# First tile's heads first in the key stage, two query blocks moved to the gather stage, inputs loaded at once

## The reference, cut to what matters

```python
q = (xc @ wq).reshape(C, 8, 2, 128)              # 16 half-heads of 128
s = einsum('chpd,hpnd->chpn', q, sub_keys)       # 128 scores a half-head
s1, i1 = top_k(s[:, :, 0], 16); s2, i2 = top_k(s[:, :, 1], 16)
top, pos = top_k((s1[..., :, None] + s2[..., None, :]).reshape(C, 8, 256), 16)
g = softmax(top)                                 # 8 heads x 16 = 128 experts a token
a = gelu(einsum('chkd,cd->chk', u_tab[eidx], xc))
out = einsum('chk,chkd->cd', g * a, v_tab[eidx])
```

## Time and profile before

| | us |
|---|---|
| runs timed (3) | 3694.53 median, 3687.42 to 3694.57 |
| profiled execution | 3679.2 |
| its span, first to last instruction | 3677.4 |
| TensorE's mean granted clock | 0.870 of full |

### The profile page before, as it was taken

The page is one execution under the profiler, slowest core; times in us unless marked ns, Lnnn a source line. Parts: engine busy times, 40 slices in busy tenths (PEclk is TensorE's granted clock), DMA queues, the critical chain, the costliest instruction groups (busy, mean ns, idle before and its releaser), DMA issues. The chain is left out here.

```text
span 3677.4 us, 30576 instructions
## 1 busy us (share of the span) xinstructions
PE 2689.4 (73%) x8773; PEld 1376.5 (37%) x8773; DVE 2342.6 (64%) x5334; ACT 694.0 (19%) x1885; POOL 1482.5 (40%) x1582
## 2 busy tenths in 40 slices
PE   6998676766697666863086886197417799999998
PEld 3445532223372232211022472042102265566555
DVE  1233877778876778789855468887886536433542
ACT  1021100312122200310022220022002213410341
POOL 0000365665546655676664006656666600000000
PEclk8999878986899878886599987599658999999999
DMA  8656699999999999999998349999999953234322
GB/s 307 240 194 225 248 403 389 352 360 333 400 360 369 355 395 403 363 370 360 370 368 311 105 151 378 407 387 381 383 407 364 362 207 132 92 138 141 141 92 75
DMA packets 345650, 1086.52 MB, mean 295 GB/s; under 512 B 32657, under 2 KB 41357, under 8 KB 338189
## 3 DMA queue, kind: packets, MB, share of 16 engines
q0 software_dynamic: 227216, 849.45, 60.4%
q1 hardware_dynamic: 118268, 235.12, 18.1%
HBM read 1080.21 MB, written 4.24 MB: 295 GB/s over the span
## 5 line engine op out<-in xcount | busy, mean ns | idle before, releaser
L2447 ACT ACTIVATE heads<-common,dots 128x128 f32<-128x128 f32 x768 | 277.9, 396 | 731.3 <-PE psum L2463 359.0
L1214 PE MATMUL psum<-ring,turned 128*128 128x512 f32 (+1 forms) x800 | 356.1, 598 | 75.0 <-issue 56.5
L2503 POOL DMA_INDIRECT lent<-in_peer_u_dram,picks_u x274 | 258.2, 942 | 351.2 <-DVE picks_u L2199 168.1
L2413 DVE SCALAR_TENSOR_TENSOR lent<-lent,psum 128x1024 f32<-128x1024 f32 x274 | 325.1, 1218 | 41.2 <-issue 20.5
L2463 PE MATMUL psum<-proj,heads 128*128 128x512 f32 x374 | 207.0, 655 | 181.4 <-DVE turned L2413 129.1
L2463 PE MATMUL psum<-lent,heads 128*128 128x512 f32 x524 | 285.6, 653 | 70.8 <-DMA lent<-in_peer_v_dram,picks_u 24.1
L2503 POOL DMA_INDIRECT lent<-in_peer_v_dram,picks_u x262 | 248.0, 947 | 133.8 <-issue 63.7
L1884 PE MATMUL psum<-ring,turned 128*128 128x512 f32 x512 | 243.1, 635 | 39.4 <-issue 13.4
L2421 DVE SCALAR_TENSOR_TENSOR psum<-lent,dots,psum 128x512 f32<-128x512 f32 x262 | 197.9, 755 | 101.4 <-DMA lent<-in_peer_v_dram,picks_u 55.0
L1214 PEld LDWEIGHTS psum<-ring,turned 128*128 128x128 f32 x800 | 161.5, 204 | 265.5 <-issue 253.3
L2413 DVE SCALAR_TENSOR_TENSOR proj<-proj,psum 128x1024 f32<-128x1024 f32 x195 | 232.7, 1218 | 37.7 <-issue 13.8
(11 more groups left out here) (416 smaller groups left out, 4698.3 us busy)
## 6 DMA issues: line engine op xcount, KB each, us to landing
ring<-in_w_in_dram SPq DMA_DIRECT2D x37, 2048.0 KB
ring<-in_peer_wq_dram SPq DMA_DIRECT2D x10, 2048.0 KB
lent<-in_w_in_dram SPq DMA_DIRECT2D x9, 2048.0 KB, 8.4
ring<-in_w_out_dram SPq DMA_DIRECT2D x9, 2048.0 KB
proj<-in_ada_w_dram POOLq DMA_DIRECT2D x14, 1024.0 KB, 6.7
heads<-in_ada_w_dram POOLq DMA_DIRECT2D x13, 1024.0 KB, 7.1
gate_rows<-in_ada_w_dram POOLq DMA_DIRECT2D x13, 1024.0 KB, 7.1
lent<-in_w_out_dram SPq DMA_DIRECT2D x5, 2048.0 KB, 8.1
```

The source lines that it names most:

```text
L1214: mm = pe.matmul(psum[:, b % nb, 0:cols], lhs(k, it), w[:, kk, :], start=k == 0, stop=k == k_total - 1)
L2413: dve.scalar_tensor_tensor(out=src, in0=src, scalar=1.0, in1=kept_row, op0=ALU.mult, op1=ALU.mult, accum_out=weight).then_inc(rows_used.se ...
L2447: act.activation(diags[n % DIAGS], ident, ACT.Copy, scale=dots[:, j:j + 1]).then_inc(diag_ready.sem, 1)
L2503: pool.indirect_dma_start(out=row_slot(r), out_offset=None, in_=tables_dram[which], in_offset=bass.IndirectOffsetOnAxis(ap=picks_u[:, t, j ...
```

## The change

1. **Setup.** SP issues the two x tiles right after `common`, then the small rows, then the two ctx tiles, then the ring loads; before, x and ctx were issued at the start of the ada stage and SP waited for them before the fourth ada load. The fourth ada load gets a place of its own (`proj`), so that all four are issued in the setup stage. The squares of all tiles, the scaling and the turning of stream 0 move into the setup stage. All 23 small loads are issued in the projection stage. Of 16 modulating steps DVE now makes ten and ACT six (8 and 8 before).
2. **Modulation pairs.** Projection (1,3,5,7) to (3,6,9,12); attention (4,18) to (4,9,14,18); output projection (1,3) to (1,2,3); norm (0) and key stage (3,8) to none.
3. **Key stage** for stream 0 (`TILE_FIRST`): 24 items in six groups; the groups that turn the rows back are put behind items 15, 17, 19 and 21; the last picks are made at the stage's end.
4. **`queries_left`**: heads 8 to 15 of tile 1 as a guest at the start of the experts stage; query blocks 2 and 3 are released there.
5. **Row slots.** Three (five) rows are issued as soon as the first picks are known, four more once block 0 is used; slots 4, 5 and 10 are held until `queries_left` is done.

```diff
+    beside_ring[len(plan) - 1] = (RING, proj[:, 0:SLOT], None, False)
...
             sp.dma_start(common, io["common"]).then_inc(*packs_loaded.one(16))
+            for t in range(2):
+                sp.dma_start(stream[:, t, :], io["x"][0, t * P:t * P + P, :]).then_inc(*latents_loaded.one(16))
...
+    TILE_FIRST = ((0, 0), (1, 0), (1, 1), (2, 0), (0, 1), (3, 0))
+    LEFT_OVER = (2, 3)
+    BLOCK_FIRST = ((0, 0), (1, 0), (2, 0), (3, 0), (3, 1))
...
-        split = (3,)
-        items = [(4 * b + j, t, n) for b in range(4) for t, n in (((0, 1), (1, 1)) if b in split else ((0, 2),)) for j in range(4)]
+        order = BLOCK_FIRST if hosted() else TILE_FIRST
+        items = [(4 * b + j, t, 1 if (b, 1) in order else 2) for b, t in order for j in range(4)]
...
+        rows_at = [15 + 2 * n for n in range(len(rows_back))]
...
+                if i in rows_at:
+                    turn_row_back(pe, rows_at.index(i))
             dot(pe, last)
-            turn_rows_back(pe)
+            used.extend(freed[b] for b in range(4) if hosted() or b not in LEFT_OVER)
...
+            if not hosted():
+                pair_indices(dve, 2 * s, PEER_HEADS - 2)
+                dve.wait_ge(*step_v.now())
+                write_picks(dve, l, 2 * s, 2 * TOPK, PICKS)
...
+    def queries_left(l):
...
+        heads_left = [4 * b + j for b in LEFT_OVER for j in range(4)]
...
+                for k in range(KD):
+                    mm = pe.matmul(psum[:, i % 3, 0:P], w[:, k, (h % 4) * P:(h % 4) * P + P], turned_s[0][:, k, P:2 * P],
+                                   start=k == 0, stop=k == KD - 1)
...
+                yield 2.0, asked_at(i)
...
+    HELD = (4, 5, 10)
+    first_order, all_order = [6, 7, 8, 0, 1, 2, 3, 9], [2, 3, 4, 5, 6, 7, 8, 0, 1, 9]
+    late_order = [6, 7, 8, 11, 12, 0, 1, 2, 3, 9]
...
-        quads.host(project_, (1, 3, 5, 7))
+        quads.host(project_, (3, 6, 9, 12))
...
-        quads.host(attend, (4, 18))
+        quads.host(attend, (4, 9, 14, 18))
...
-        quads.host(out_, (1, 3))
-        quads.host(norm, (0,))
+        quads.host(out_, (1, 2, 3))
+        quads.host(norm)
         wq0 = len(used) + 1
-        quads.host(keys, (3, 8), then_rows=lambda pool: rows_beside_keys(pool, wq0, 4))
+        quads.host(keys, then_rows=lambda pool: rows_beside_keys(pool, wq0, 3, 7))
```

More of the change, by code:

```diff
@@ L553, in sync @@
                     r += n
+            for t in range(2):
+                sp.dma_start(stream[:, 2 + t, :], io["ctx"][0, t * P:t * P + P, :]).then_inc(*loaded.one(16))
             issue_loads(sp)
@@ L775, in scalar @@
             act.wait_ge(*read_a.at(4))
-            for k in range(KD):
+            for k in range(2, KD):
                 x = turned_s[1][:, k, :]
@@ L2051, in vector @@
             dve.wait_ge(*step_v.now())
+            if not hosted():
+                pair_indices(dve, 2 * s, PEER_HEADS - 2)
+                dve.wait_ge(*step_v.now())
+                write_picks(dve, l, 2 * s, 2 * TOPK, PICKS)
         def first_of(h):
-            return items.index((h, 0, 1 if h // 4 in split else 2))
+            return min(i for i, (head, t0, _) in enumerate(items) if head == h and t0 == 0)
         def asked_at(i):
@@ L2080, in scalar @@
                        .then_inc(*read_a.one())
-            for n, (t, g) in enumerate(rows_back):
-                act.wait_ge(*products.at(4 + dots_at(last) + n + 1))
-                act.copy(mixed_v[:, t, 512 * g:512 * g + 512], psum[:, n, :]).then_inc(*scaled.one())
+                if i - 1 in rows_at:
+                    n = rows_at.index(i - 1)
+                    t, g = rows_back[n]
+                    act.wait_ge(*turned_back.at(n + 1))
+                    act.copy(mixed_v[:, t, 512 * g:512 * g + 512], psum[:, 6 + n % 2, :]).then_inc(*copied_back.one())
             if l == 1:
@@ L2089, in keys_stage @@
         if l == 0:
-            lifted_free[s] = products.now()
+            lifted_free[0] = products.now()
     heads_hi = heads[:, 2048:4096]
@@ L2526, in experts_stage, with gather @@
         gather_count[0] += 1
-        def gather(pool, row, tile0, first, picked0, early):
+        def gather(pool, row, tile0, first, picked0, early, held=None):
             r, back = first + row, row_before[first + row]
+            if held and slot_no[r] in HELD and slot_no[r] not in slot_no[first:r]:
+                pool.wait_ge(*held)
             t, which, j = tile0 + row // (2 * PICKS), row // PICKS % 2, row % PICKS
@@ L2547, in gpsimd @@
             for row in range(ahead, 4 * PICKS):
-                gather(pool, row, 2 * s, first, picked0, s == 0)
+                gather(pool, row, 2 * s, first, picked0, s == 0, left_done[-1] if len(left_done) > left_before else None)
             if follows is not None:
```

241 lines of the change are left out of this document (139 added, 102 removed).

## The result

The changed kernel takes 3754.34 us (median of 4 runs, 3740.38 to 3760.61) against 3694.16 of before (4 runs): ratio 1.0162, 95% interval 1.0131 to 1.0193. It is slower by 60 us; the forecast was 23 us slower and its range ended at 3733.

What follows compares the result with a forecast made beforehand. The prediction took DMA to bound the gather stages, PE the stretch from 50 to 409 us, loads the first 50. Its terms summed to +23.1 us on the profiled 3679.2, giving 3702.3, or 3717.6 for a median; range 3692 to 3733.

Steps and rivals of the forecast that it cites:

- Part 1, the start: Up to the projection's first pair: earlier loads, fewer ACT columns and no wait for that pair's load, -12.4 us in sum.
- Part 2, the pairs: Modulation pairs at new places: +7.7 us in projection and branch stages, +6.6 in attention, +2.0 in output projection.
- Part 3, the key stage: Layer 0's key stage: blocks 2 and 3 stay 256 wide, opening copy +1.3 us, DMA late by +2.9.
- Part 4, the two loads: Two weight loads a layer go in beside the gathered rows: +2.5 us in layer 0, +9.3 in layer 1.
- Part 5: Layer 1's key stage and experts opening: same items, no pair to drop, row 10 waits for row 0's use, +4.5 us.
- Narrow blocks: Rival, key stage: blocks 2 and 3 are only 128 columns wide, saving 15.1 us a layer, -7.1 in sum; chance 0.08.
- DMA has room: Rival, first 50 us of rows: DVE or POOL sets the pace, the loads cost nothing, +8.5 us in sum; chance 0.14.
- Pairs covered: Rival, projection, branches and attention: PE waits anyway, so the pairs' waits cost 14.3 us less, +8.8 in sum; chance 0.10.
- Held slots late: Rival, experts stage: `queries_left` stays at the lower clock, held slots come 9 us late a layer, +41 in sum; chance 0.08.

Runs made afterwards that it cites:

- start_only: The kernel before with the new start (the diff's "Setup" parts) alone; pairs, key stage and row slots as before: 3565.64 us against 3569.77, ratio 0.9992.
- the second pair of traces: Both kernels unchanged, measured once more on one chip: kernel before 3691.09 us in its one run, changed kernel 3754.18 against 3696.24, ratio 1.0172.
- the first comparison: The changed kernel against the kernel before, as first measured and traced: 3754.34 us against 3694.16, ratio 1.0162.
- narrow: The changed kernel with key-stage blocks 2 and 3 made 128 columns wide for tile 0 alone: 3594.69 us, ratio 1.0068 to the kernel before.
- late_loads: Changed kernel without `queries_left`, full ring, no seam, query blocks 2 and 3 released in the gather stage by a tiny guest: 3724.81 us, 1.0057 of before.
- the first group: Experiments made on one chip with the kernel before (3569.8 us there): new start alone, start with pairs, changed kernel without `queries_left`, and with narrow items.
- seam_in_before: The kernel before with the seam alone: row 643 takes slot 9, which row 639 has just taken: 3709.70 us against 3697.26, ratio 1.0039.
- after_again: The changed kernel, unchanged, measured once more on the same chip as the kernel before: 3754.18 us against 3696.24, ratio 1.0172.
- start_pairs: The kernel before with the new start and the modulation pairs at their new places; key stage and row slots as before: 3578.89 us, ratio 1.0019.
- before_again: The kernel before, unchanged, measured once more for a trace from the experiments' chip: 3691.09 us in its one run.

## Why the prediction was right in sign and wrong in size

**Part 1, the start: right.** Forecast -11.1 by the start of the projection (10.1 + 1.0), measured -12.0. The first pair, three groups into the projection, does not wait (products at 61.56 and 62.44 us), as forecast (-1.3). With the old places the loads that the start brings forward meet the first pair's: start_only shows that half of the gain is lost at once. The forecast had not asked what the earlier start makes late.

**Part 2, the pairs: the failed step, mis-sized.** "Back-to-back pairs stall PE 4.5 us" took the shortest landing, 5.0 us. The load took 8.1, and the stall was 7.60; the one in the branch stage was 1.60, less than the 2.6 forecast. The granted clock was 0.57 over the stretch behind, with products of nearly twice the time, which the sum had nowhere. Up to the key stage the forecast was +3.9 and the second pair of traces shows +13.8 (the first one +13.6: 346.26 against 332.64). By the traces of the first comparison, the projection and branch stages lose 12.2 us, so that the merge stage's first product comes at 116.76 against 116.56 and the start's gain is gone; the forecast had them lose 6.4 (7.7 less 1.3). In the attention stage the waits were 0.36 + 0.81 + 1.42 = 2.6 us, as forecast (0.6 + 0.6 + 1.4), yet the stage grew by 8.7 instead of 6.6; 1.6 of the difference are slower products at its start (231.05 to 234.77, in before 230.85 to 232.93). From there to the key stage it is 4.8 instead of 2.0. The Trainium skill ("TensorE: Matmul & The Clock Gate", Part 1) has the throttle follow sustained activity; the row of 90 to 110 us agrees, 0.57 where PE was busy 10.65 of 20 us.

**Part 3, the key stage: right.** From its first product to the opening copy 82.1 us (before 82.2: 332.64 to 414.80), forecast 1.3 longer; the second pair of traces has 82.1 against 79.8, 2.3 longer. The width of the items, read from the expression, held, and narrow shows that it is worth 15.1 us a layer, as the rival said.

**Part 4, the two loads: right in layer 1, open in layer 0.** late_loads isolates them: about 9 us in layer 1, forecast 9.3. In layer 0 they cost nothing that is left from row 576 to row 704 and at most 3.4 at row 1024, forecast 2.5. The 6.7 us that the changed kernel loses there up to row 576 are not shown to be theirs: they hang on one pair of traces, and narrow's 16.5 on the chip of the first group are more than late_loads shows for the loads.

**Part 5: right.** 3.1 us measured, 3.3 to 4.5 forecast.

**What the sum lacked: the seam.** "Row slots" was costed at its start only. The seam alone costs 12 to 14 us (seam_in_before, shown by itself), and taking it out of the changed kernel gives 12 to 22; on the faster chip of the first group it costs 1 to 2. Beside the pairs it is the second step that failed: the sum had it at nothing, it lies in a place that no stage boundary marks, and no rival named it. The pairs' excess of some 10 us and the seam's 12 to 14 together make nearly all of the 25.7 us between the forecast and the second pair of traces.

**The rivals.** Narrow blocks: did not happen, price confirmed. DMA has room: refuted by late_loads in layer 1. In layer 0 DMA did have room, by row 576. (The terms of this rival add up to +8.4, not +8.5.) Pairs covered: refuted, they cost more. Held slots late: in layer 0 the rows are 29.0 us late at row 32 and 14.8 at row 64, below the 16.1 of row 0; so the delay is real, 13 us and not 9, and is given back. Likely this is because before has its own hole at 440 to 450 us, while after has one at 460 to 470 with a DMA share of 0.71. On the slower chips it can't be seen in the total. But on the chip of the first group the guest with its held slots and late loads costs 16.5 us in layer 0 (narrow), where late_loads has 0 to 3.4 for the loads; the rest falls to the held slots, to the heads made again, or to the 13 rows by which the guest shifts all guests behind it. Which of them it is was not tried, so this rival is open, not refuted.

The terms now: 13.8 + 2.3 + 6.7 + 14.3 + 3.1 + 8.6 = 48.8 us, the distance of the two traces. The medians of the same runs are 58 apart, as the profiled run of after_again was its fastest. The 9 us between the two figures are within the scatter of single runs (3739 to 3759) and are put down to no cause. The sum closes because it is read from one pair of traces; of its terms only those of the pairs, the seam and layer 1's rows come back in other traces.

## What to carry to other kernels

When a ring's order is changed in one stretch, write down for every entry how many entries ago its slot was last used, across the places where two orders meet: one distance of 4 among 10s and 13s cost 12 us by itself on one chip, though hardly anything on a faster one. A load that is brought forward competes with the next load in line, so place its first consumer by when that one lands, not by the old step number: one group later, the branch stage started 11.7 us earlier than before instead of 5.4. And a stall of TensorE is priced with the slower products behind it.

## What was not expected of the hardware

The chip of the first group ran the kernel before in 3569.8 us (19 runs, 3563.7 to 3575.7), those of all other comparisons in 3694 to 3703: 3.5 to 3.7% apart, well beyond the scatter on either. The difference lies in the gather stages, where the one moved 389 GB/s at a DMA share of 1.00 and the other 368 at 0.97, in the same stretch of the same code; before them there is little: with the same start and pairs the key stage's first product is at 345.61 us on the one (start_pairs) and 347.89 on the other (after_again). The 409 GB/s of the earlier trace rows is what both reach in their best slices.

What differs shows in DVE's pauses over 460 to 1930 us. In start_only those that no load and no other engine's result ended (the profile puts them down to "issue", "remote" or DVE's own instruction before) add up to 2 us, in before_again to 107. The rows of that stretch are nearly as much apart: start_only is 1.4 us ahead of before_again at row 0 and 91.0 at row 1023. The seam's price on the slower chips is made of such pauses too. What DVE waits for in them is not shown, nor why the one chip has none.

A microsecond count of a gather kernel is thus comparable on one chip only, and the seam shows that the price of a single change can differ between chips as well.
